# Modulating the first projection's input: the scale moves from VectorE to ScalarE, the rounding becomes an instruction of its own

## The reference

```
(shift, scale, gate) x 2 = SiLU(cond) @ w_ada + b_ada        # per group: context or latent
h = RMSNorm(x) * gain * (1 + scale1) + shift1
p = h @ w_in                                                 # first projection, then the three branches
```

## Time and profile before

| | us |
|---|---|
| median of 3 runs (lowest, highest) | 2398.67 (2397.53, 2400.23) |
| profiled execution, its own time | 2402.82 |
| its span, first to last instruction | 2401.0 |
| mean granted TensorE clock | 0.963 |
| TensorE busy | 2188.6 |
| VectorE busy | 1483.2 |
| ScalarE busy | 1143.3 |

### The profile page before, as it was taken

One profiled execution on the slowest core, in us unless ns is written; L12 is line 12 of the kernel. 1 busy time (PEld: TensorE's weight loads), 2 busy tenths in 40 slices (PEclk: granted clock), 3 DMA queues, 4 the chain that ended last, 5 costly groups with the idle time before them and its releaser, 6 DMA issues. The chain is left out here.

```text
span 2401.0 us, 28904 instructions
## 1 busy us (share of the span) xinstructions
PE 2188.6 (91%) x11236; PEld 1892.9 (79%) x11236; DVE 1483.2 (62%) x2021; ACT 1143.3 (48%) x1534; POOL 8.2 (0%) x12
## 2 busy tenths in 40 slices
PE   7799999999999999998899969965999999999993
PEld 4499988977777899997799968855877777777772
DVE  6967576346544444443544444555678879879984
ACT  6733565333444434332343333332567667667760
POOL 1000000000000000000000000000000000000000
PEclk9899999999999999998999989997899999999996
DMA  9844333433333455543355555520589889889981
GB/s 353 288 148 140 105 139 102 138 123 119 114 115 113 149 179 183 176 167 110 125 182 180 188 177 193 181 90 21 206 287 339 297 287 345 278 309 336 333 294 55
DMA packets 127287, 459.92 MB, mean 192 GB/s; under 512 B 15456, under 2 KB 17280, under 8 KB 126880
## 3 DMA queue, kind: packets, MB, share of 16 engines
q1 hardware_dynamic: 127136, 457.92, 55.3%
HBM read 453.88 MB, written 3.98 MB: 191 GB/s over the span
## 5 line engine op out<-in xcount | busy, mean ns | idle before, releaser
L161 DVE TENSOR_TENSOR wlo<-raw,whi 128x1024 fp32r<-128x1024 f32 x832 | 1006.5, 1223 | 734.7 <-ACT whi L155 720.0
L155 ACT ACTIVATE whi<-raw 128x1024 fp32r<-128x1024 f32 x832 | 870.6, 1058 | 918.6 <-PE bank L173 669.7
L171 PE MATMUL bank<-hhi,whi 128*128 128x384 f32 x1664 | 567.2, 341 | 29.1 <-DVEq L1519 16.9
L173 PE MATMUL bank<-hhi,wlo 128*128 128x384 f32 x1664 | 559.8, 336 | 0.0
L172 PE MATMUL bank<-hlo,whi 128*128 128x384 f32 x1664 | 559.4, 336 | 0.0
L171 PEld LDWEIGHTS bank<-hhi,whi 128*128 128x128 f32 x1664 | 315.2, 189 | 48.5 <-issue 24.9
L172 PEld LDWEIGHTS bank<-hlo,whi 128*128 128x128 f32 x1664 | 315.1, 189 | 1.8
L173 PEld LDWEIGHTS bank<-hhi,wlo 128*128 128x128 f32 x1664 | 314.6, 189 | 0.0
L1994 PE MATMUL bank<-whi,group_hi 128*128 128x512 f32 x512 | 203.6, 398 | 5.3 <-DVE wlo L161 4.0
L1996 PE MATMUL bank<-wlo,group_hi 128*128 128x512 f32 x512 | 201.5, 394 | 0.0
L1995 PE MATMUL bank<-whi,group_lo 128*128 128x512 f32 x512 | 200.5, 392 | 0.0
(11 more groups left out here) (320 smaller groups left out, 2414.6 us busy)
## 6 DMA issues: line engine op xcount, KB each, us to landing
raw<-in_dense SPq DMA_DIRECT2D x448, 512.0 KB, 3.7
raw<-in_moe SPq DMA_DIRECT2D x384, 512.0 KB, 5.0
merged<-in_x SPq DMA_DIRECT2D x8, 768.0 KB, 6.4
cs_rows_bc<-cs_rows SPq DMA_DIRECT2D x8, 768.0 KB, 5.0
out_y<-merged SPq DMA_DIRECT2D x4, 768.0 KB, 3.3
pool_w_sb<-in_pool_w SPq DMA_DIRECT2D x1, 1024.0 KB, 6.2
w_router_sb<-in_w_router SPq DMA_DIRECT2D x1, 1024.0 KB, 4.5
pool_inv_count<-in_pool_inv SPq DMA_DIRECT2D x1, 768.0 KB, 4.3
```

Of the source, the lines that this page charges most:

```text
L155: self.nc.scalar.activation(self.whi[:, n % W, :], self.raw[:, n % R, :], ACT.Copy).then_inc(self.hi_done, 1)
L161: self.nc.vector.tensor_tensor(self.wlo[:, n % W, :], self.raw[:, n % R, :], self.whi[:, n % W, :].bitcast(F32), ALU.subtract).then_inc(se ...
L171: self.nc.tensor.matmul(out, self.whi[:, s, c], xhi[:, k, :], start=(k == 0), stop=False)
L173: last = self.nc.tensor.matmul(out, self.wlo[:, s, c], xhi[:, k, :], start=False, stop=(k == blocks - 1))
```

## The change

VectorE's `mix` multiplies by `rstd` only, in one instruction over both token groups. ScalarE's `mix_high` applies scale (mod_a) and shift in place in `tmp`, one instruction for each group, waits for them on a new semaphore `mix_h`, and rounds to `hhi` in one Copy over both groups. VectorE's `mix_low` subtracts once over both groups. `s_t`, `s_mhi` and `s_mlo` count one for each block instead of two, and the waits on them are halved to name the same blocks.

```diff
@@ def sp (Scan) @@
-        sp.wait_ge(self.s_mixed, 2 * KB)
+        sp.wait_ge(self.s_mixed, KB)
@@ scalar @@
             def mix_high(k):
 
-                act.wait_ge(s_t, 2 * k + 2)
+                act.wait_ge(s_t, k + 1)
                 for g, (a, b) in enumerate(SEG):
-                    A(N.hhi[:, k, a:b], tmp[:, k % 4, a:b], ACT.Identity, bias=N.mods[:, k, g:g + 1], scale=1.0)\
-                        .then_inc(s_mhi, 1)
+                    A(tmp[:, k % 4, a:b], tmp[:, k % 4, a:b], ACT.Identity, bias=N.mods[:, k, g:g + 1], scale=N.mod_a[:, k, g:g + 1])\
+                        .then_inc(s_mh, 1)
+                act.wait_ge(s_mh, 2 * k + 2)
+                A(N.hhi[:, k, :], tmp[:, k % 4, :], ACT.Copy).then_inc(s_mhi, 1)
@@ vector @@
                 if k >= 4:
-                    dve.wait_ge(s_mlo, 2 * k - 6)
-                for g, (a, b) in enumerate(SEG):
-                    V.scalar_tensor_tensor(out=tmp[:, k % 4, a:b], in0=xt[:, k, a:b], scalar=N.mod_a[:, k, g:g + 1],
-                                           in1=N.rstd[:, a:b], op0=ALU.mult, op1=ALU.mult).then_inc(s_t, 1)
+                    dve.wait_ge(s_mlo, k - 3)
+                V.tensor_tensor(tmp[:, k % 4, :], xt[:, k, :], N.rstd[:, :], ALU.mult).then_inc(s_t, 1)
 
             def mix_low(k):
 
-                dve.wait_ge(s_mhi, 2 * k + 2)
-                for g, (a, b) in enumerate(SEG):
-                    V.scalar_tensor_tensor(out=N.hlo[:, k, a:b], in0=tmp[:, k % 4, a:b], scalar=N.mods[:, k, g:g + 1],
-                                           in1=N.hhi[:, k, a:b].bitcast(F32), op0=ALU.add, op1=ALU.subtract).then_inc(s_mlo, 1)
+                dve.wait_ge(s_mhi, k + 1)
+                V.tensor_tensor(N.hlo[:, k, :], tmp[:, k % 4, :], N.hhi[:, k, :].bitcast(F32), ALU.subtract).then_inc(s_mlo, 1)
@@ tensor @@
                 if s < 2:
-                    pe.wait_ge(s_mlo, KB * (s + 1))
+                    pe.wait_ge(s_mlo, KB // 2 * (s + 1))
```

More of the change, by code:

```diff
@@ L712, in mix_phase @@
         sem("ada_" + n) for n in ("squares", "sqsum", "row", "tr", "four", "add")]
-    s_t, s_mhi, s_mlo = [sem("mix" + n) for n in ("_t", "_hi", "_lo")]
+    s_t, s_mh, s_mhi, s_mlo = [sem("mix" + n) for n in ("_t", "_h", "_hi", "_lo")]
     s_ld, s_pads, s_dhi, s_dlo, s_dt = [sem("sin_" + n) for n in ("loads", "zero", "dthi", "dtlo", "dt")]
@@ L1005, in mix_phase @@
     N.tile0 += tiles + 2 * blocks
-    nc.clear_and_free_semaphores([loaded, s_tanh, s_silu, s_chi, s_clo, s_zero, consts_in, x_in, s_sq, s_sqsum, s_t, s_mhi, s_mlo,
+    nc.clear_and_free_semaphores([loaded, s_tanh, s_silu, s_chi, s_clo, s_zero, consts_in, x_in, s_sq, s_sqsum, s_t, s_mh, s_mhi, s_mlo,
                                   s_ld, s_pads, s_dhi, s_dlo, s_dt, s_conv, s_fin, s_xtanh, s_zt])
```

## The result

The changed kernel takes 2409.81 us (median of 7, 2406.32 to 2413.76), the kernel before 2398.67 (median of 7, 2396.72 to 2404.43). The ratio is 1.0041 with a 95% interval of 1.0028 to 1.0055, or 6.7 to 13.2 us slower, 9.8 in the middle. The forecast was 2407.8, 9.1 slower. The profiled execution has a span of 2409.0.

A forecast was written before the change was run, and what follows sets the result against it. The prediction took the round trip through ScalarE, nearly equal to VectorE's list, to bound the loop. Loop 6.0, last four blocks 1.65 and clock 1.5 made 9.1 us on 2398.67: 2407.8, range 2402 to 2413.

The forecast's parts named there:

- What bounds the loop: Conditioning product beside the mixing: the round trip through ScalarE sets the 3.71 us period, within 0.11 of VectorE's list.
- the trip: From one mix through ScalarE's mix_high and `whi` and VectorE's `wlo` to the next mix: 3.71 us, forecast 4.25.
- Rival 1: In the loop VectorE's list decides and ScalarE has slack: about -3 us, 2395.7; chance 8%.
- The second pointer: ScalarE's Identity reading scale as well as bias from [128,1] operands: 0.091 us more each, bounds 0 and 0.091.
- rival 2: The second [128,1] operand on ScalarE's Identity is free: +4.6 to +6.1 us, 2403.3 to 2404.8; chance 17%.
- The loop: Mixing slots beside the conditioning product: +0.54 us a block, together +6.0, bounds 3.7 and 6.0.
- the layout: Loop slots laid out one after another with the new durations: `wlo` lags 2.0, 3.9, then 6.0 us after successive groups.
- rival 4: TensorE's clock falls further, among the conditioning tiles: up to 3.9 us more, 2411.7; chance 15%.
- The last four blocks: Behind slot 63, blocks 12 to 15: second projection tile starts 1.65 us later, bounds 0.9 and 1.7.
- The clock behind the pause: TensorE's pause before the second projection tile grows to 3.75 us and costs the upper level: +1.5, bounds 0 and 1.5.
- The sum: Whole kernel: 6.0 + 1.65 + 1.5 = 9.1 us slower, 2407.8.
- Rival 3: Part of the loop's delay is absorbed between the groups, no fall of the clock: about +4 us, 2402.7; chance 10%.

The follow-up runs named there:

- act_part: Changed kernel with VectorE's old instruction pairs for mix and mix_low put back; 3091.82 us, not usable as expert tile loads rose from 384 to 768.
- direct: Changed kernel without ScalarE's wait and Copy, Identity writing the rounded high part itself (low part not the reference's); ratio to the kernel before 0.9994 (0.9980 to 1.0007).
- later_after: Changed kernel with mix_high and mix_low each one slot later; ratio to the kernel before 1.0016 (1.0006 to 1.0026).
- vec_part: Changed kernel with ScalarE reduced to one Copy a block, scale and shift left out of the result; ratio to the kernel before 0.9968 (0.9955 to 0.9981).
- tail_before: Changed kernel with blocks 12 to 15 made as in the kernel before on both engines; ratio to the kernel before 1.0028 (1.0015 to 1.0041).
- warm: Changed kernel with 16 extra unused matmuls in TensorE's pause before the second projection tile; ratio to the kernel before 1.0035 (1.0020 to 1.0049).
- later_before: Kernel before with mix_high and mix_low each one slot later; ratio to the kernel before 0.9995 (0.9986 to 1.0003).
- no_scale: Changed kernel with a constant 1.0 for the scale operand of ScalarE's Identity; ratio to the kernel before 1.0014 (1.0003 to 1.0025).
- later_tail: Changed kernel with mix_high and mix_low one slot later and the last four blocks as before; ratio to the kernel before 1.0002 (0.9993 to 1.0011).
- later_warm: Kernel before with mix_high and mix_low one slot later and ten extra unused matmuls before the second projection tile; ratio 0.9985 (0.9975 to 0.9994).

## Why the prediction was right

*What bounds the loop.* Right, and shown in three ways: the period follows ScalarE's length with VectorE fixed (4.44 in act_part), stays at 3.70 with less VectorE work (direct), and the loss in the loop all but vanishes when the trip is opened (later_after, 7.0 of 7.1). Rival 1, VectorE's list, would have made the kernel 3 us faster. Its condition (ScalarE adds less than 0.29 a block) is met in vec_part, and there it happens.

*VectorE.* Forecast -5.8 of busy time, -5.7 measured; 552 ns instead of 557.

*ScalarE.* Forecast 1.43 a block, 1.44 measured. The second pointer at its upper bound was right (92 to 93 ns), which removes rival 2. The Copy took 524 instead of 510, the wait 0.02 to 0.03.

*The loop.* Forecast +6.0; 7.1 measured. Up to tile 62 it is the layout's: `wlo` at 126.31 for 120.29, 5.8 net of the 0.2 at the start. The rest came in the last two conditioning tiles, whose matmuls ran at 0.63 (127.58 to 131.2): a piece of rival 4, the clock, which I had priced and not taken. In tail_before and warm the loop is 6.7 longer, and the piece lies elsewhere: nothing is lost in the last two tiles, but 0.9 between the second and the third group, where the granted clock from 100 to 106 us was 0.72 in both and 1.00 in the changed kernel. So the layout's 5.8 comes back in all three, and 0.9 to 1.3 more goes with a fall of the clock, at a place that varies.

*The last four blocks.* Forecast +1.65, 1.68 measured, and 0 in tail_before.

*The clock behind the pause.* Forecast +1.5, 1.56 measured, and 0 in warm. The size was right; my reason, that a pause of 2.1 keeps the level and one of 3.0 loses it, was too simple, as later_before shows.

*The sum.* 7.1 + 1.7 + 1.6 = 10.4 at L413 against 9.1. The whole time says 9.8 (6.7 to 13.2). The profiled pair shows only 8.0 at the end. On the way the lag, counted from the first `wlo`, moves by more than that: it is 12.0 in the tile that the kernel before reaches at 510 us and 7.3 in the one at 588, back at 10.6 by 1720, and then shrinks again. The largest step lies where the kernel before was granted 0.93 (500 to 600 us) and the changed one 0.98. The change has no part in that code, and nine of the other ten profiles have 0.97 or 0.98 there too; no_scale has 0.93. So the profile of the kernel before was slow in that place. That the whole time came within 0.7 us of the forecast is partly luck: the loop lost 1.1 more than forecast, and clock differences far behind it are larger than that. Rival 3, a delay taken up between the groups, did not occur in the changed kernel: after the second group `wlo` stands at 100.18 for 96.22, and at the head of the third at 109.28 for 105.31, 4.0 both times (0.2 of it from the start).

## What to carry to other kernels

An engine with idle time on average can still have none at the place where work is moved to: follow one item through all engines, add up the trip, and compare it with each engine's own list before calling any of them the bound. When two of these lie within a few per cent, as 3.60 and 3.71 here, relieving the one does not pay for loading the other: here the period grew by the 0.72 added to the trip less the 0.18 that mix saved in it, and the 0.36 taken from VectorE's list bought nothing. Starting a step one slot later, so that nobody waits for what was only just made, recovered 7.0 of 7.1 us here without less work; it made the change harmless, not useful.

## What the runs showed of the hardware

A second [128,1] operand on a ScalarE instruction cost as much as the first: 91 ns for the first (491 to 582 ns) and 92 to 93 for the second (396 to 489 ns at 128 columns, 494 to 586 at 256). Applying scale and shift in two short instructions for two token groups pays four of them a block. A ScalarE instruction that waits for the semaphore of the one before it started 0.02 to 0.03 us after that one's end, where neighbours without a wait overlap by 0.09.

Equal pauses of TensorE can end differently. Before the second projection tile, after 2.08 to 2.11 us the upper level stayed in the kernel before, in tail_before and in later_tail, while in later_before it was gone for 3.2 us (131.43 to 134.63). After 3.00 to 4.15 us it was lost in all four kernels that paused so long (changed, act_part, no_scale, later_after), and after 0.31 to 1.53 us it stayed in all four that did (vec_part, direct, warm, later_warm). Each of these is one profile. What differed ahead of the equal pauses was not found.
